# Down-projection of a hybrid decoder step: the low parts of the fetched product tiles made by GpSimd in place of VectorE

## What is computed

```python
def conv_ffn(h, st, w_in, wc, w_down):
    z = h @ w_in
    g, st_new = causal_dwconv(z[..., :D_FF], st, wc)
    return (jax.nn.silu(g) * z[..., D_FF:]) @ w_down, st_new
```

## Time and profile before

| | |
|---|---|
| median of the 3 runs shown | 2599.93 us (2598.96 to 2603.32) |
| the profiled execution, its own time | 2608.27 us |
| its span (first to last instruction) | 2606.5 us |
| mean granted TensorE clock in it | 0.991 |
| busy: TensorE, VectorE, ScalarE, GpSimd | 2531.8, 1655.7, 802.5, 968.2 us |
| L808 (down-projection, both layers) | 3150 matmuls, 509.0 us |

### The profile page before, as it was taken

How to read it: one execution, slowest core, us unless ns; L and a number is a source line. 1 busy time by engine, 2 the same in 40 slices (tenths; PEclk the granted TensorE clock), 3 DMA queues, 4 the chain that set the end, 5 groups by cost and what they waited for, 6 DMA issues and landing times.

```text
span 2606.5 us, 41678 instructions
## 1 busy us (share of the span) xinstructions
PE 2531.8 (97%) x17036; PEld 2375.7 (91%) x17036; DVE 1655.7 (64%) x2593; ACT 802.5 (31%) x1402; POOL 968.2 (37%) x635
## 2 busy tenths in 40 slices
PE   8999998999999999999999999989899999999997
PEld 8999988999999999987777777759899999999997
DVE  6999777666666555655555555564766666665555
ACT  5111343333333211333333333343433333331112
POOL 1000126777777322321010101124277777752222
PEclk9999999999999999999999999999999999999998
DMA  4111102455444544444444444433077778775321
GB/s 152 41 41 41 44 17 66 141 141 143 145 139 160 194 163 146 172 147 146 143 148 147 141 167 146 165 108 121 25 267 267 269 273 291 267 276 183 99 83 67
DMA packets 106557, 383.93 MB, mean 147 GB/s; under 512 B 23936, under 2 KB 41216, under 8 KB 103936
## 3 DMA queue, kind: packets, MB, share of 16 engines
q1 hardware_dynamic: 106368, 381.26, 43.3%
HBM read 339.15 MB, written 176.04 MB: 198 GB/s over the span
## 4 chain that ended last, share of the span: by engine, by line
PE 89%; DVE 7%; issue 2%; ACT 1%; DMA 1%; POOL 0%; DVEq 0%; SPq 0%; ACTq 0%
PE reg L949 29%; PE reg L808 20%; PE reg L775 12%; PE reg L1061 9%; PE ob L949 3%; PE reg L1041 3%; PE ob L1097 3%; PE reg L881 2%; PE reg L1014 1%; PE reg L1082 1%; PE ob L1082 1%; PE reg L1150 1%; PE reg L1137 1%; DVE neg_s L2299 1%; DMA w_raw<-in_wstream 1%
## 5 line engine op out<-in xcount | busy, mean ns | idle before, releaser
L949 PE MATMUL reg<-xo,wq 128*128 128x352 f32 x5280 | 862.6, 324 | 24.7 <-ACT part L1288 11.5
L949 PEld LDWEIGHTS reg<-xo,wq 128*128 128x128 f32 x5280 | 852.4, 189 | 28.2 <-ACT part L1288 12.1
L808 PE MATMUL reg<-hid,w_sp 128*128 128x352 f32 x3150 | 509.0, 323 | 0.0
L808 PEld LDWEIGHTS reg<-hid,w_sp 128*128 128x128 f32 x3150 | 508.7, 188 | 0.0
L488 POOL TENSOR_TENSOR w_sp<-w_raw,w_sp 128x1024 fp32r<-128x1024 f32 x63 | 173.9, 2763 | 739.3 <-ACT w_sp L483 718.8
L1837 DVE TENSOR_TENSOR h<-reg,h 128x1056 f32<-128x1056 f32 x199 | 250.1, 1257 | 274.1 <-PE reg L808 226.7
L775 PE MATMUL reg<-xs,w_sp 128*128 128x352 f32 x2016 | 332.5, 326 | 10.2 <-DVE xs L1826 9.8
L775 PEld LDWEIGHTS reg<-xs,w_sp 128*128 128x128 f32 x2016 | 328.1, 189 | 13.6 <-issue 13.1
L1714 POOL TENSOR_TENSOR wq<-wqr,wq 128x512 fp32r<-128x512 f32 x168 | 235.1, 1410 | 164.6 <-DVE wqr L2066 164.6
L1714 POOL TENSOR_TENSOR wq<-w_raw,wq 128x512 fp32r<-128x512 f32 x168 | 255.5, 1531 | 94.9 <-ACT wq L1275 94.8
L1061 PE MATMUL reg<-xs,w_sp 128*128 128x352 f32 x1512 | 279.6, 332 | 0.4 <-DVE VT L2281 0.4
(11 more groups left out here) (249 smaller groups left out, 2946.3 us busy)
## 6 DMA issues: line engine op xcount, KB each, us to landing
w_raw<-in_wstream SPq DMA_DIRECT2D x192, 512.0 KB, 4.3
out_sv<-in_cache_v SPq DMA_DIRECT2D x16, 4088.0 KB, 16.7
out_sk<-in_cache_k SPq DMA_DIRECT2D x16, 4088.0 KB, 16.8
kvr<-in_kva SPq DMA_DIRECT2D x16, 2048.0 KB, 9.1
kvr<-in_kvb SPq DMA_DIRECT2D x16, 1536.0 KB, 6.9
hid_spill<-tmp SPq DMA_DIRECT2D x44, 528.0 KB, 5.4
hraw<-hid_spill SPq DMA_DIRECT2D x44, 528.0 KB, 4.5
wt<-in_wtab SPq DMA_DIRECT2D x16, 512.0 KB, 4.4
```

Of the source, the lines that this page charges most:

```text
L808: mm = nc.tensor.matmul(out[:, t, :], w[:, wh, kk * 512 + m * P:kk * 512 + (m + 1) * P], hid[:, par_g, kk, xh, t * TS:(t + 1) * TS], start ...
L949: mm = nc.tensor.matmul(out, w[:, wh, k * P:(k + 1) * P], xo[:, o, 1 - xh if o == X_T3 else xh, k, :], start=(first and k == 0 and wh + xh ...
```

## The change

The function `hidden_lo` moves from VectorE's program to GpSimd's, with the same operands and the same semaphores. On GpSimd the two of group 0 stand behind the split of unit (0,0), and the two of group g+1 each behind one `lo_after` of group g.

```diff
@@ GpSimd
+                def hidden_lo(g, c):
+                    pool.wait_ge(hid_hi, NJ * L + 2 * g + c + 1)
+                    nc.gpsimd.tensor_tensor(hid[:, g % 2, c, 1, :], hraw[:, g % 2, c, 1, :],
+                                            hid[:, g % 2, c, 0, :].bitcast(F32), ALU.subtract).then_inc(hid_lo, 1)
+
...
                     else:
                         split_lo(pool, down_unit(L, 0, 0))
+                        hidden_lo(0, 0)
+                        hidden_lo(0, 1)
                         history(j)
                         silu_scale(j)
                         split_lo(pool, down_unit(L, 0, 1))
...
                 for g in range(NG - 1):
                     for x in range(2):
                         lo_after(pool, down_unit(L, g, x))
+                        hidden_lo(g + 1, x)
@@ VectorE
-
-                def hidden_lo(g, c):
-                    dve.wait_ge(hid_hi, J0 + 2 * g + c + 1)
-                    nc.vector.tensor_tensor(hid[:, g % 2, c, 1, :], hraw[:, g % 2, c, 1, :],
-                                            hid[:, g % 2, c, 0, :].bitcast(F32), ALU.subtract).then_inc(hid_lo, 1)
...
-                    if not more:
-                        hidden_lo(0, 0)
                     combine(j, 3)
-                    if not more:
-                        hidden_lo(0, 1)
...
-                            if (x, m) in ((0, 3), (1, 1)):
-                                hidden_lo(g + 1, x)
```

## The result

The changed kernel takes **2754.36 us** (median of 4, 2752.84 to 2756.35) against 2601.62 us for the kernel before (median of 4, 2598.96 to 2609.72): ratio 1.0577, 95% interval 1.0561 to 1.0593. It is slower by 152.7 us; forecast were 159 us and 2759, in a range of 2734 to 2781.

The account below looks back on a forecast made before the run. TensorE was taken to bound the down-projection stage. Waits of 119 us, 40 us of lost clock and 0.3 us at the entry sum to 159 us, giving 2759 us, in a range of 2734 to 2781.

Parts of the forecast that it names:

- What bounds the kernel: Down-projection stage: TensorE alone sets the time; a microsecond it waits is lost, one taken off VectorE is worth nothing.
- The place in the queue: GpSimd's product (g+1,1) stands behind a split awaiting group g's end, so TensorE waits at the start of group g+1.
- The length of the chain: From group end through ScalarE's high part, GpSimd's split and product to TensorE's restart: a wait of 6.26 us.
- The count: Group boundaries where TensorE waits: 10 in layer 0, 9 in layer 1; 19 x 6.26 = 119 us.
- The clock: TensorE's clock falls in each gap and slows the matmuls after it: 2.1 us a gap, 40 us in all.
- the low end of the term: Clock loss after the gaps: every other gap escapes, the others cost 1.61 us, giving 0.8 us a gap.
- The entry: Start of each layer's stage, group 0's products behind the split of unit (0,0): 0.3 us for both layers, between 0 and 3.
- The other signs: Profile after: VectorE's busy time down 55 us, GpSimd's up about 86, splits near 2.40 us, both stages' mean clock near 0.9.
- The sum: Whole kernel: 119 + 40 + 0.3 = 159 us slower, 2759 us.
- The clock that holds: Rival: the waits at the group boundaries come but TensorE's clock does not fall; 2719 us, chance 0.07.
- The rival of no wait at all: GpSimd runs ahead, so product (g+1,1) is done before group g ends; 2600 us, within 0.2%, chance 0.01.

Follow-up runs that it names:

- first experiment: The changed kernel with product (g+1,1) ahead of the split of unit (g+2,0), all products still on GpSimd: 2607.43 us, ratio 1.0000.
- the second products alone: The kernel before with only products (g+1,1), 20 of the 44, on GpSimd behind the second split as in the change: 2755.08 us, ratio 1.0570.

## Why the prediction was right

**What bounds the kernel** held. TensorE had no idle time in the stage, and every microsecond put in its way was paid in full: 152.6 us of growth in the two stages against 152.7 between the medians. Work taken off VectorE brought nothing (first experiment: 55 us of work moved, ratio 1.0000).

**The place in the queue** was the cause, and the only one. It holds with the work on GpSimd at another place (no loss), with half of it (all or none of the loss, by the half), and with the work on VectorE at a late place (86 us lost).

**The length of the chain.** 6.26 us was computed from start to start; the trace has 882.60 - (853.23 + 144 x 0.1616) = 6.10 us, and 5.99 us of idle time. The parts were 0.21 from the end of the group to ScalarE's start, 1.14 from there to GpSimd's, 2.29 from there to the product's and 2.46 more to TensorE's restart; split and product were each some 0.05 us shorter than taken (2.34 and 2.41). The term of 119 us measured 116, or 113.8 as idle time.

**The count** of 19, with no gap ahead of the last group of layer 1, was exact.

**The clock.** 40 us were taken and 38.7 found as busy time. That nearness is partly luck. The price from the two long gaps of the kernel before (1.88 and 2.63 us) was sound, and the groups spread around it, from 1.4 to 2.9 us. But the low end of the term, that every other gap escapes, rested on one gap of 3.01 us that cost nothing, and was wrong: none of the 20 gaps of 2.5 us and none of the 19 of 3.4 us escaped. It also rested on two short gaps where the kernel before has three. The third, of 2.99 us, cost as well:

```profile
396.14 11.44 PE L949 MATMUL reg<-xo,wq 128*128 128x352 f32 x60 [2.99 <-DVE wq L2075]
...
396.14:407.42 11.28, 11.28 (x61) 0.85 0.20 58
```

60 matmuls should take 9.70 us and took 11.28, at a mean clock of 0.85: 1.58 us, so that two of three paid and not one of two.

The sentence of the Trainium skill that was weighed (TensorE: Matmul & The Clock Gate, "HAM oscillation — how this bites in real kernels"), that such a loop pays in every round, is what the trace shows: in both layers every group behind a gap of 5.99 us took at least 24.80 us.

**The entry.** 0.3 us was taken; alone it measured a ratio of 0.9999. In the changed kernel the pair of products runs beside VectorE like this:

```profile
847.40 5.57 POOL L1738 TENSOR_TENSOR hid<-hraw,hid 128x1056 fp32r<-128x1056 f32 x2
...
848.27 2.36 DVE L2122 TENSOR_TENSOR g<-g,rst 128x704 f32<-128x704 f32 x1
...
850.98 2.54 DVE L2133 TENSOR_SCALAR acc<-g,pt 128x1024 f32<-128x1024 f32 x1
```

The scaling takes 2.36 us (0.89 before), the first tap takes 2.54 (0.74 before), while the two products together take only 0.67 us over 2 x 2.45 and end at 852.97, 0.26 us before TensorE is there. The trace has the second product start at 849.83 and last 3.15 us; the scaling ends at 850.63, 0.8 us after that start, about its length when alone. So the engines take turns here. The trace agrees with the rule of the Trainium skill (SBUF — State Buffer, "SBUF: two separate sides"), that the port pair of the two is an exclusive lock. By even stretching (7.1 us for both, as the prediction has it) the end would have been 854.5.

**The other signs.** GpSimd's busy time rose by 86.9 us (86 forecast) and its splits fell from 2763 to 2424 ns in the mean over the kernel. VectorE's fell by 46.3, not 55: the scaling and the first tap are longer by 3.3 us in layer 0, as shown above, and by 3.6 us in layer 1. The mean clock of the two stages is 0.89 and 0.90 (near 0.9 forecast), by these windows, of which the first ends 29 us before the stage does:

```profile
853.23:1160.00 306.77, 251.29 (x1442) 0.89 0.35 122
2399.66:2727.60 327.94, 274.01 (x1585) 0.90 0.25 85
```

**The sum** was 6 us too large: 3 us in the length of the chain, counted from start to start, and the rest in the clock term counted the same way (152.6 - 116 = 37 and not 40).

**The rivals.** The clock that holds was made to hold by 6 filling matmuls and then gave 2724 us, near the 2719 computed for it. The rival of no wait at all is the first experiment's kernel: once the product stands ahead of the split, the time is that of the kernel before. No version ran faster than the kernel before beyond the noise; what the change frees on VectorE has no use in this stage.

## What to carry to other kernels

When work moves to another engine's queue, ask first what the instruction ahead of it waits for. If that is an event of the very engine that needs the result, a chain has been tied behind it, however idle the new engine is: GpSimd stood still for 6.8 us ahead of the split that made TensorE wait. The cure is the order, not the speed. A gap of a few microseconds that returns in every round cost TensorE its clock on top here, a third of the wait again, and halving the gap didn't give that back; filling all but 0.85 us of it did.

## What was not expected of the hardware

The clock's price does not follow the length of the gap: 1.67 us for 2.5 us of idle time, 2.41 for 4.9, 2.04 for 6.0, 2.36 for 8.4, and 1.84 for 3.4 us behind 2.7 us of filling work. It varies instead from round to round: in the changed kernel gaps of the same 5.99 us were followed by groups of 24.80 and of 26.27 us, next to each other. The order is not random: in both layers the groups go down from 25.8 or 25.9 us to 24.80, jump to 26.27 and go down again, and the kernel with the second products alone does nearly the same (25.97 down to 24.80, then 26.31). What decides it was not tried.

Nor do length and place decide whether a single short gap costs anything. In the kernel before, one gap of 3.01 us had cost nothing. In the changed kernel the same wait, of the same 3.01 us, is paid for (the 60 matmuls run 11.28 us until the next piece starts at 1952.38, where 9.70 are due):

```profile
1941.10 11.44 PE L949 MATMUL reg<-xo,wq 128*128 128x352 f32 x60 [3.01 <-DVE wq L2083]
```

Over the profiles of all twelve kernels of this document this wait cost the clock in eight and nothing in four, and the one of 2.9 us at the start of layer 0's block cost it in nine (24 matmuls in 5.65 to 5.68 us) and nothing in three (4.13 or 4.14). In rounds of 27.5 and 31 us, gaps of 2.5 and 3.4 us cost it in every group of both layers.
